# Hosted steps moved by a few positions in a fused three-block kernel

## The reference

```python
def first_block(x, ...):                       # DEPTH = 2
    for l in range(DEPTH):
        h = rms_norm(x, norm1[l])
        proj = h @ w_in[l]                     # four groups of 4 heads
        # A: latent attention: rms_norm of a_cq, a_ckv, then @ mla_w_uq, @ mla_w_ukv, rope
        # B: window of 128 with sinks: rope(b_q), rope(b_k), b_v
        # C: per query the 128 keys with the highest index score
        #      score[t, s] = sum_h w[t, h] * relu(qi[t, h] . ki[s])
        # D: causal attention with forget gates
        x = x + concat(o_a, o_b, o_c, o_d) @ w_out[l]
        h2 = rms_norm(x, norm2[l])
        x = x + square(relu(h2 @ w_up[l])) @ w_down[l]
    return rms_norm(x, final_norm)

def second_block(x, c, ...):                   # one layer
    h = rmsnorm(x, norm_g) * (1 + scale) + shift   # from c @ w_ada
    # three groups of 8 heads with dilated windows and a bias by distance (rel_bias),
    # merged by their softmax weights; a pooling branch; both gated, then @ w_out
    return rmsnorm(x, final_g)
```

## Time and profile before

| | before |
|---|---|
| median of 3 runs | 1847.85 us |
| lowest to highest | 1845.85 to 1849.39 us |
| profiled execution | 1847.98 us |
| its span, first to last instruction | 1846.2 us |
| mean granted clock of PE | 0.995 |
| PE busy | 1791.2 us, 97% |
| DVE busy | 925.3 us, 50% |
| POOL busy | 727.7 us, 39% |
| ACT busy | 659.6 us, 36% |

### The profile page before, as it was taken

How to read it: one execution, slowest core, us unless ns; L and a number is a source line. 1 busy time by engine, 2 the same in 40 slices (tenths; PEclk the granted TensorE clock), 3 DMA queues, 4 the chain that set the end, 5 groups by cost and what they waited for, 6 DMA issues and landing times.

```text
span 1846.2 us, 22975 instructions
## 1 busy us (share of the span) xinstructions
PE 1791.2 (97%) x9055; PEld 1460.9 (79%) x9057; DVE 925.3 (50%) x1508; ACT 659.6 (36%) x1230; POOL 727.7 (39%) x328
## 2 busy tenths in 40 slices
PE   8999899999999999999999999999999999999997
PEld 8677668888888886776688888888788988888786
DVE  4679762514232346697627362727522134339374
ACT  4533552322122235345523131222435343442212
POOL 3233434445444433333444444544343434334442
PEclk9999999999999999999999999999999999999999
DMA  7224002232233232220025434243242223223221
GB/s 231 69 69 164 9 24 91 77 107 92 91 102 102 68 94 99 69 69 1 24 69 183 174 100 160 91 165 100 82 148 69 91 69 118 67 69 96 87 69 46
DMA packets 104448, 171.00 MB, mean 93 GB/s; under 512 B 21616, under 2 KB 39432, under 8 KB 103209
## 3 DMA queue, kind: packets, MB, share of 16 engines
q1 hardware_dynamic: 103320, 169.79, 28.1%
q10 hardware_dynamic: 1040, 0.00, 0.0%
HBM read 166.56 MB, written 7.93 MB: 95 GB/s over the span
## 4 chain that ended last, share of the span: by engine, by line
PE 82%; DVE 8%; issue 5%; POOL 2%; ACT 2%; DMA 0%; SPq 0%; DVEq 0%; POOLq 0%; ACTq 0%
PE G L2090 24%; PE G L2092 23%; PE G L2091 23%; POOL w_lo L1323 2%; PE S L2374 2%; PE S L1094 1%; DVE select L1930 1%; PE G L2410 1%; DVE work L1766 1%; DVE neg_max L1966 1%; PE S L1068 1%; DVE top L1765 1%; PE G L2358 1%; PE S L1079 1%; PE G L2391 1%
## 5 line engine op out<-in xcount | busy, mean ns | idle before, releaser
L1323 POOL TENSOR_TENSOR w_lo<-raw,w_hi 128x1024 fp32r<-128x1024 f32 (+2 forms) x268 | 657.6, 2475 | 986.6 <-ACT w_hi L1369 674.6
L2090 PE MATMUL G<-h_hi,w_hi 128*128 128x512 f32 x896 | 356.1, 397 | 4.0 <-POOL w_lo L1323 2.1
L1369 ACT ACTIVATE w_hi<-raw 128x2048 fp32r<-128x2048 f32 (+1 forms) x94 | 178.9, 1903 | 492.6 <-PE G L2092 492.6
L2092 PE MATMUL G<-h_hi,w_lo 128*128 128x512 f32 x896 | 350.0, 391 | 0.0
L2091 PE MATMUL G<-h_lo,w_hi 128*128 128x512 f32 x896 | 349.5, 390 | 0.0
L2090 PE MATMUL G<-w_hi,h_hi 128*128 128x512 f32 (+2 forms) x704 | 277.6, 394 | 3.7 <-DVE line L1758 1.4
L2092 PE MATMUL G<-w_hi,h_lo 128*128 128x512 f32 (+2 forms) x704 | 267.7, 380 | 0.0
L2091 PE MATMUL G<-w_lo,h_hi 128*128 128x512 f32 (+2 forms) x704 | 267.3, 380 | 0.0
L2090 PEld LDWEIGHTS G<-h_hi,w_hi 128*128 128x128 f32 x896 | 168.5, 188 | 42.4 <-issue 4.4
L2092 PE MATMUL G<-w_hi,u_lo 128*128 128x512 f32 x512 | 199.2, 389 | 0.0
L2090 PE MATMUL G<-w_hi,u_hi 128*128 128x512 f32 x512 | 199.2, 389 | 0.0
(11 more groups left out here) (317 smaller groups left out, 2217.9 us busy)
## 6 DMA issues: line engine op xcount, KB each, us to landing
raw<-in_w_in_dram SPq DMA_DIRECT2D x40, 1024.0 KB, 5.2
raw<-in_w_up_dram SPq DMA_DIRECT2D x32, 1024.0 KB, 5.2
raw<-in_w_down_dram SPq DMA_DIRECT2D x32, 1024.0 KB, 5.0
raw<-in_w_out_dram SPq DMA_DIRECT2D x12, 1024.0 KB, 5.0
w_ada<-in_w_ada_dram SPq DMA_DIRECT2D x4, 3072.0 KB, 11.9
skew_scratch<-line_scratch SPq DMA_DIRECT2D x1, 4608.0 KB
raw<-in_w_in_dram SPq DMA_DIRECT2D x8, 512.0 KB, 4.2
raw<-in_w_in_dram SPq DMA_DIRECT2D x4, 832.0 KB, 6.5
```

The costliest lines, as they stand in the source:

```text
L1323: ins = pool.tensor_tensor(w_lo[:, c % SPLIT_SLOTS, part, 0:n], raw[:, c % RAW_SLOTS, part, 0:n], w_hi[:, c % SPLIT_SLOTS, part, 0:n].bitc ...
L1369: act.activation(w_hi[:, c % SPLIT_SLOTS, :, 0:n], raw[:, c % RAW_SLOTS, :, 0:n], ACT.Copy).then_inc(high_ready, 1)
L2090: pe.matmul(dst, a_hi, b_hi, start=first, stop=False)
L2092: return pe.matmul(dst, a_lo, b_hi, start=False, stop=last)
```

## The change

Five edits of places; the number of instructions stays the same on each engine.

1. `parted(n)`: behind the third unit of `K`, PE and ACT take one more step before the scores of the first window. `side_steps` counts it; the number of steps that DVE's top-k rounds are spread over (`EARLY_STEPS`) stays.
2. Job B: the fourth index round moves from position 1 to 2, and the steps of `L` and `U` are spread from 13 on instead of 12. `L` stands at 16 (15 before), `U` 0 to 2 at 20, 24, 28 (19, 23, 27), `U` 3 stays at 31. In job C, with five steps instead of four, K stands at 17 (18 before), its third unit at 21, the first window's scores at 24 (both at 22 before), the turned probabilities at 28 (27), the output at 31 as before.
3. Second block: the first step of each of the three groups stands three positions sooner (5 instead of 8, in the last group 4 instead of 7).
4. ACT's squares before the feed-forward part stand one behind each of the last four `high_T`.
5. PE waits for `line_ready` at the first hosted step of job A (position 18), not before the job.

```diff
+def parted(n):
+    return n > 0 and SIDE[n - 1][0] in ("K",)
...
-    return sum(continues(n) + (n > 0 and SIDE[n - 1][0] == "P") for n in range(first, end))
+    return sum(continues(n) + parted(n) + (n > 0 and SIDE[n - 1][0] == "P") for n in range(first, end))
...
-          JOB_B: {1: 1, 6: 1, 11: 1, **spread(12, 32, side_steps(0, AT["K",]))},
+          JOB_B: {2: 1, 6: 1, 11: 1, **spread(13, 32, side_steps(0, AT["K",]))},
...
-EARLY_STEPS = side_steps(1, AT["M",]) - 1
+EARLY_STEPS = side_steps(1, AT["M",]) - sum(parted(n) for n in range(NS)) - 1
...
 def host_steps(jobs, items, first, end):
-    for pos, count in spread(first, end, 2 * items + 1).items():
+    places = {pos: count for pos, count in spread(first, end, 2 * items + 1).items() if count}
+    first_place = min(places)
+    places[first_place - 3] = places.pop(first_place)
+    for pos, count in places.items():
         HOSTED2[jobs[pos // 32]][pos % 32] = count
...
# side() of ACT and of PE, ahead of "if n < NS:"
+                        if parted(n):
+                            yield
...
                 ahead(OUT_JOB + 1, 1)
-                high_T(gain2, tr + TR_NORM2, HALF_K, KT)
+                act.wait_ge(bank_drained, unit + (TT * FFN_JOB + UNITS_CREDIT))
                 for t in range(TT):
-                    act.wait_ge(bank_drained, unit + (TT * (OUT_JOB + 1) + t + 1 + UNITS_CREDIT))
+                    high_T(gain2, tr + TR_NORM2, HALF_K + t, HALF_K + t + 1)
                     ins = square_sum(t)
...
                 def side():
 
+                    if l == 0:
+                        pe.wait_ge(line_ready, 1)
                     pe.wait_ge(idx_rows_ready, l + 1)
...
                     ins.then_inc(line_filled, 1)
-                    pe.wait_ge(line_ready, 1)
```

## The result

| | before | after |
|---|---|---|
| median | 1848.62 us (4 runs) | 1834.07 us (4 runs) |
| lowest to highest | 1845.85 to 1850.73 us | 1833.28 to 1836.06 us |
| profiled execution, span | 1846.2 us | 1832.0 us |
| mean granted clock in it | 0.995 | 0.996 |
| PE busy | 1791.2 us, 97% | 1787.4 us, 98% |

After over before is 0.9922 (95% interval 0.991 to 0.9933): 14.55 us less by the medians, and 14.2 us less in the two spans. I had forecast 1837.0 us and a range of 1834.5 to 1842.0. The direction is right; the median lies 2.9 us under the forecast (1837.0 - 1834.07) and 0.43 us under the range.

A forecast was written before the change was run, and what follows sets the result against it. TensorE, busy 97% of the span, was taken as the bound. Waits removed, 1.44 + 1.45 + 1.36 + 2.12 + 2.1 + 2.4 = 10.9 us, took 1847.98 us (median 1847.85) to 1837.0 us, range 1834.5 to 1842.0.

The forecast's parts named there:

- What bounds the kernel: Whole kernel: TensorE is busy 97% of the span, so only some of the 55 us it stands still can be won.
- key step too early: Job C: the key step meets a delayed VectorE rotation, TensorE waits 0.9 us in both layers, 1838.8 us; chance 0.07.
- moved waits: Hosted steps: VectorE's chain sets the pace, so latent step, keys and scores give nothing, 1842.9 us; chance 0.11.
- round 4: Job B's index round at position 6: TensorE reaches it 0.68 us sooner and newly waits there, so nothing is won.
- VectorE did not become the bound: Denies the slower rival: VectorE paces jobs C, D and V, 30 more window-step waits, 29 us, 1866 us; chance 0.03.
- Line table and the clock behind it: Start of job A: TensorE's 1.44 us stop goes, and with it the half-clock stretch behind it, 1.45 us.
- Job B: Index round and latent step one position later: 0.68 us less waiting at the latent step, twice, 1.36 us.
- Keys parted: Job C: three positions between third key unit and first scores remove TensorE's 1.06 us wait, twice, 2.12 us.
- covers: Job C's spare time before TensorE would wait: 1.2 us at the key step, 0.5 us at the first window's turn.
- Norm squares: Start of the feed-forward part: ScalarE's split 3.0 us sooner, so TensorE's wait for GpSimd goes, 2.1 us in two layers.
- First scores: Second block: scores three positions sooner remove TensorE's 1.23 us wait for the exponentials in two groups, 2.4 us.
- Rival (1): The clock still falls near job A or elsewhere, 1.45 us, 1838.4 us; one other fall fewer gives 1835.5; chance 0.20.

## Why the prediction was right and where it was off

**The step that failed** is the price of two stops, and the room for the clock at the lower end of the range. The mechanism held: each wait that was to go went, and the one that was to appear appeared. But the sum took the bracket's idle time as the price of the stops for GpSimd's split and for the first scores, 2.1 + 2.4 us, and they gave 2.68 + 2.83. That is 1.0 us, and with it the forecast would have been 1836.0, still inside the range. The lower end, 1834.5, left room for little more than one fall fewer. In the profiled pair falls at other places gave 1.55 us and the first data 0.44, and the first median came out at 1834.07. That last step below the range is luck of the draw: over all 14 executions the mean is 1835.1. The points one by one:

**What bounds the kernel**: right. TensorE's stops lie on the path: in the traces each stop that was taken away came back in full behind it, and none was moved to another engine. The three mechanisms against it did not come: no key step too early, no moved waits beyond round 4, and VectorE did not become the bound (the window outputs wait as before, 1.9 us in all).

**Line table and the clock behind it**: 2.95 us for 2.89 in the profiled pair, and that is in part luck. I took the fall as gone in full, from one profile; it stands behind the stop in four profiles of seven, so on average this term is worth 0.8 us of clock (an estimate, 4/7 of 1.45), and the profile read here was one of the four.

**Job B**: right in each wait: round 3 none, round 4 0.68, L 0.34 (forecast 0.7 and 0.3), 0.68 us a layer.

**Keys parted**: right, 2 x 1.06, with the covers at 1.19 and 0.79 us (forecast 1.2 and 0.5).

**Norm squares**: the mechanism was right, the term mis-sized: 2.1 us forecast, 2.68 measured as 1.36 + 1.32 at the stops. My step "TensorE waited 1.1 us for it, 2.1 in two layers" took the bracket for the price. GpSimd's split ended 1.93 us ahead of need (forecast 2.0), so the cover was sized right.

**First scores**: the same error, 2.4 forecast, 2.83 measured. Together the two terms are 1.0 us short. (At the keys the gap of 1.06 us was the whole price, 1.07 measured. There short transposes stand ahead of the stop; at the two others it is a product of 512 columns, whose row reaches 0.16 us over the start of the next.)

**The range** was too narrow on the side of the clock. Rival (1) had one fall fewer at 1835.5, and I set the lower end 1.0 us below that. The profiled pair had 1.55 us from falls at other places and 0.44 us from the first data, both luck, besides the 1.0 us just named: 10.9 + 1.0 + 1.55 + 0.44 = 13.9 of 14.2; the small remainder of the table is the rest. Over many executions it is 11.4 us at equal clock (forecast 9.45, that is 10.9 without the fall) and 2.2 us of clock (forecast 1.45). The part of the 11.4 above the stops' 10.5 us (1.50 + 3.46 + 2.68 + 2.83) is not settled; the single parts show an excess of the same kind, 1.5 us in their sum. Why the clock rose by more than the one place explains is open too: each shorter stop may spare a fall now and then, or 14 executions still drew well; no run here tells these apart.

## What to carry to other kernels

Where one engine is 97% busy, each of its stops can be priced from the timeline, but from start to start and not by the idle time in the bracket: a stop behind a stream of overlapping matmuls cost 0.15 to 0.3 us more than its gap. A wait that is taken away upstream moves whatever the waiting engine releases: before moving a wait, list the transfers and splits that hang on that engine's progress, and ask which chain on another engine does not move with them. When single edits are worth 1 to 3 us and the clock falls a few times per execution, at places that differ from one to the next, compare mean times at equal clock, or rows within the trace, not single medians; and give the range room for the clock on both sides.

## What the runs showed of the hardware

- A stop of 1.44 us was followed by a fall of TensorE from 2.4 to 1.2 GHz in four profiles of seven; filled with idle work (one profile) or gone (eight), in none. A stop of 1.88 us at the start of the second block was followed by one in 12 profiles of 15.
- A fall of 3.41 us cost 1.1 to 1.5 us where TensorE is busy. In the sparse products of the second block one of 3.41 us cost 0.05 to 0.2 us (10.77 to 10.94 us for the stretch in five profiles, 10.72 without a fall). Where it lasted 6.83 us, in six profiles, the stretch took 12.4 us.
- Mean clock and time go together at 1.33 us per 0.001 over all kernels and runs; the kernel before ranges from 1844.5 to 1852.7 us, most of that by the clock.
- A VectorE operation of four columns took 2.21 us instead of 0.17 while GpSimd ran a subtraction of 128 x 1024 (2.4 us).
